# A gate's sigmoid rewritten as a tanh, its sum and its half moved into vector products

## The reference, cut to what matters

```python
# first block, end of the mLSTM branch: the output gate
hn = ((h - mu) * lax.rsqrt(var + EPS)) ... * norm_g
return jax.nn.sigmoid(o_pre) * hn                 # 512 channels

# second block, three branches mixed, each with its own gate of 1024 channels
y = sigmoid(g_a) * (short_conv @ w_sc_out)        # "ya"
  + sigmoid(g_b) * (stick_breaking @ w_sb_out)    # "yb"
  + sigmoid(g_c) * (ssm @ w_ssm_out)              # "yc"
h = y @ w_o
```

## Time and profile before

| | |
|---|---|
| time, median of 3 runs | 902.93 us (901.65 to 908.4) |
| the profiled execution | 907.06 us, span 905.3 us |
| PE busy | 860.5 us (95%) |
| DVE busy | 651.4 us (72%) |
| ACT busy | 503.7 us (56%), of it 43 table loads in the program |
| mean granted clock of PE | 0.97 of full |

### The profile page before, as it was taken

How to read it: one execution, slowest core, us unless ns; L and a number is a source line. 1 busy time by engine, 2 the same in 40 slices (tenths; PEclk the granted TensorE clock), 3 DMA queues, 4 the chain that set the end, 5 groups by cost and what they waited for, 6 DMA issues and landing times.

```text
span 905.3 us, 15843 instructions
## 1 busy us (share of the span) xinstructions
PE 860.5 (95%) x6396; PEld 810.8 (90%) x6396; DVE 651.4 (72%) x1011; ACT 503.7 (56%) x723; POOL 7.6 (1%) x17
## 2 busy tenths in 40 slices
PE   8899997999899999999997999999899899999997
PEld 7789986889799999999997899898899899999886
DVE  5765787678567988887867896787798766665553
ACT  5643447455447666655455756777657554444342
POOL 0200000000000000000000000000000000000000
PEclk9999999989998999999998999999999799999999
DMA  9974556756062665667862376455575177775751
GB/s 339 244 216 138 171 182 195 215 172 229 28 185 72 214 186 185 187 196 240 261 210 70 118 251 185 147 187 181 169 233 166 60 250 225 233 233 186 168 204 47
DMA packets 139592, 166.89 MB, mean 184 GB/s; under 512 B 5520, under 2 KB 123280, under 8 KB 139520
## 3 DMA queue, kind: packets, MB, share of 16 engines
q1 hardware_dynamic: 137712, 162.82, 57.0%
q0 software_dynamic: 720, 2.02, 1.2%
q10 hardware_dynamic: 1088, 1.05, 0.3%
HBM read 164.62 MB, written 1.25 MB: 183 GB/s over the span
## 4 chain that ended last, share of the span: by engine, by line
PE 32%; DVE 12%; ACT 8%; issue 3%; DVEq 0%; ACTq 0%
PE ps L512 32%; DVE lor L1595 5%; DVE FA L1595 3%; ACT hir L1096 2%; DVE FA L1598 1%; ACT L1434 1%; DVE INL L1595 0%; ACT X L1366 0%; DVE raw L1612 0%; ACT HIH L1372 0%; ACT FA L1434 0%; DVE FA L2256 0%; DVE FA L1601 0%; ACT FA L1476 0%; DVE X L1595 0%
## 5 line engine op out<-in xcount | busy, mean ns | idle before, releaser
L1595 DVE TENSOR_TENSOR lor<-raw,hir 128x1024 fp32r<-128x1024 f32 (+1 forms) x267 | 309.9, 1178 | 118.8 <-ACT hir L1096 112.6
L1096 ACT ACTIVATE hir<-raw 128x1024 fp32r<-128x1024 f32 (+1 forms) x257 | 260.2, 1032 | 125.1 <-PE ps L512 105.3
L512 PE MATMUL ps<-INH,hir 128*128 128x256 f32 (+1 forms) x1064 | 306.9, 288 | 4.2 <-ACT INH L1259 2.5
L512 PE MATMUL ps<-INH,lor 128*128 128x256 f32 (+1 forms) x1064 | 302.4, 284 | 2.8 <-DVE lor L1595 2.7
L512 PE MATMUL ps<-INL,hir 128*128 128x256 f32 (+1 forms) x1064 | 303.0, 285 | 1.4 <-DVE INL L1595 1.2
L512 PEld LDWEIGHTS ps<-INH,hir 128*128 128x128 f32 x1064 | 204.9, 193 | 7.4 <-issue 6.1
L512 PEld LDWEIGHTS ps<-INH,lor 128*128 128x128 f32 x1064 | 204.5, 192 | 4.9 <-DVE lor L1595 3.9
L512 PEld LDWEIGHTS ps<-INL,hir 128*128 128x128 f32 x1064 | 204.0, 192 | 2.4 <-DVE INL L1595 2.4
L512 PE MATMUL ps<-HIH,lor 128*128 128x256 f32 x688 | 195.5, 284 | 5.2 <-DVE lor L1595 5.2
L512 PE MATMUL ps<-HIH,hir 128*128 128x256 f32 x688 | 197.9, 288 | 0.0
L512 PE MATMUL ps<-HIL,hir 128*128 128x256 f32 x688 | 194.0, 282 | 0.0
(11 more groups left out here) (270 smaller groups left out, 793.6 us busy)
## 6 DMA issues: line engine op xcount, KB each, us to landing
raw<-in_w_in SPq DMA_DIRECT2D x64, 512.0 KB, 4.5
raw<-in_mod_wT SPq DMA_DIRECT2D x48, 512.0 KB, 4.5
raw<-in_ffn_w_up SPq DMA_DIRECT2D x44, 512.0 KB, 4.5
raw<-in_w_ffn_in SPq DMA_DIRECT2D x44, 512.0 KB, 4.8
raw<-in_w_ffn_out SPq DMA_DIRECT2D x22, 512.0 KB, 4.4
raw<-in_ffn_w_down SPq DMA_DIRECT2D x20, 512.0 KB, 5.0
raw<-in_xa_wkv SPq DMA_DIRECT2D x16, 512.0 KB, 3.8
raw<-in_xa_wq SPq DMA_DIRECT2D x8, 512.0 KB, 5.7
```

Source lines behind the costliest of these rows:

```text
L512: return e.matmul(o, l, r, start=start, stop=stop, skip_group_check=True)
L1096: e.activation(hi, src, ACT.Copy).then_inc(*w_hi.up(i))
L1595: return e.tensor_tensor(o, a, b, op)
```

## The change

Sigmoid(x) is written as (1 + tanh(x/2)) / 2. ACT stores t = tanh(x/2), by the scale 0.5 that an activation takes. DVE's product of gate and branch becomes (t + 1) · branch in one `stt`. The half is put in where the result is split: ACT's copy to `hi` takes scale 0.5, and DVE's `lo` is 0.5·value − `hi`, in one `stt` in place of a `tt`. For `OG`, the norm's weight, which was in the product with the gate, moves into the product ahead of it, with `rv`.

```diff
--- before.py
+++ after.py
@@ -1097,8 +1097,8 @@
 
             ahead = Ahead(plan, slot, split)
 
-            def put(x, k, n, src):
-                e.activation(x.hi[:, k:k + n, :], src, ACT.Copy).then_inc(*act.up(*x.his(k, n)))
+            def put(x, k, n, src, scale=1.0):
+                e.activation(x.hi[:, k:k + n, :], src, ACT.Copy, scale=scale).then_inc(*act.up(*x.his(k, n)))
 
             def conv(o, p, K, wname, bname, nb, i, key):
 
@@ -1150,7 +1150,7 @@
                 def o_gate(c):
                     yield from ahead.unit_g(("o", c), 8)
                     w.wait_ge(mm.at(("unit", ("o", c))))
-                    e.activation(OG[:, 2 * c:2 * c + 2, :], wide2(bank["unit", ("o", c)]), ACT.Sigmoid).then_inc(
+                    e.activation(OG[:, 2 * c:2 * c + 2, :], wide2(bank["unit", ("o", c)]), ACT.Tanh, scale=0.5).then_inc(
                         *act.up(("out", ("unit", ("o", c)))))
                     yield
 
@@ -1205,7 +1205,7 @@
                 e.activation(VR[hp], VR[hp], ACT.Sqrt).then_inc(*act.up(("deviation", hp)))
                 yield 1
                 w.wait_ge(dve.at(("OG", hp)))
-                put(mix, h0, 2, OG[:, h0:h0 + 2, :])
+                put(mix, h0, 2, OG[:, h0:h0 + 2, :], 0.5)
                 yield 1
 
             def swa(g):
@@ -1431,7 +1431,7 @@
                     yield from ahead.unit_g(("gl", c), 8)
                     dst = GLS[:, 2 * c:2 * c + 2, :] if c < 8 else GLC[:, 2 * c - 16:2 * c - 14, :]
                     w.wait_ge(mm.at(("unit", ("gl", c))), mm.at("before third norm"), dve.at("before third norm"), act.at("before third norm"))
-                    e.activation(dst, wide2(bank["unit", ("gl", c)]), ACT.Sigmoid).then_inc(*act.up(("out", ("unit", ("gl", c)))))
+                    e.activation(dst, wide2(bank["unit", ("gl", c)]), ACT.Tanh, scale=0.5).then_inc(*act.up(("out", ("unit", ("gl", c)))))
                     yield
 
                 def branch(key, c):
@@ -1503,7 +1503,7 @@
 
             def mg_put(c):
                 w.wait_ge(dve.at(("merged", c)))
-                put(mg, 2 * c, 2, GLC[:, 2 * c:2 * c + 2, :])
+                put(mg, 2 * c, 2, GLC[:, 2 * c:2 * c + 2, :], 0.5)
 
             for c in range(4):
                 ahead.unit(("yc", c), 4)
@@ -1632,9 +1632,12 @@
 
             ahead = Ahead(plan, slot, split)
 
-            def put(x, k, n, src):
+            def put(x, k, n, src, scale=None):
 
                 w.wait_ge(act.at((x.name, "hi", k + n - 1)))
+                if scale is not None:
+                    stt(x.lo[:, k:k + n, :], src, scale, x.hi[:, k:k + n, :].bitcast(F32), MUL, SUB).then_inc(*dve.up(*x.los(k, n)))
+                    return
                 tt(x.lo[:, k:k + n, :], src, x.hi[:, k:k + n, :].bitcast(F32), SUB).then_inc(*dve.up(*x.los(k, n)))
 
             def conv(o, p, K, wname, nb, i, key, *keys):
@@ -1757,11 +1760,13 @@
                 then("vc")
                 yield from across(("rv", hp), vc, DN)
                 w.wait_ge(mm.at(("rv", hp)))
-                tt(EM, EM, wide2(bank["rv", hp]), MUL).then_inc(*dve.up(("out", ("rv", hp))))
+                for h in range(2):
+                    stt(EM[:, h, :], EM[:, h, :], V("ml_norm_g", h0 + h), bank["rv", hp][:, h * T:(h + 1) * T], MUL, MUL).then_inc(
+                        *dve.up(("out", ("rv", hp))))
                 w.wait_ge(dve.last(), act.at(("out", ("unit", ("o", hp)))))
-                for h in range(2):
-                    stt(OG[:, h0 + h, :], EM[:, h, :], V("ml_norm_g", h0 + h), OG[:, h0 + h, :], MUL, MUL).then_inc(*dve.up(("OG", hp)))
-                put(mix, h0, 2, OG[:, h0:h0 + 2, :])
+                og = OG[:, h0:h0 + 2, :]
+                stt(og, og, 1.0, EM, ADD, MUL).then_inc(*dve.up(("OG", hp)))
+                put(mix, h0, 2, og, 0.5)
                 yield 1
 
             def swa(g):
@@ -2174,7 +2179,7 @@
                     yield from ahead.unit_g((key, c), 2)
                     dst = GLS[:, 2 * g:2 * g + 2, :]
                     w.wait_ge(mm.at(("unit", (key, c))), act.at(("out", ("unit", ("gl", g)))))
-                    tt(dst, dst, wide2(bank["unit", (key, c)]), MUL).then_inc(*dve.up(("branch", g), ("out", ("unit", (key, c)))))
+                    stt(dst, dst, 1.0, wide2(bank["unit", (key, c)]), ADD, MUL).then_inc(*dve.up(("branch", g), ("out", ("unit", (key, c)))))
                     yield
 
                 for c in range(4):
@@ -2279,13 +2284,13 @@
 
             def mg_put(c):
                 w.wait_ge(dve.at(("merged", c)))
-                put(mg, 2 * c, 2, GLC[:, 2 * c:2 * c + 2, :])
+                put(mg, 2 * c, 2, GLC[:, 2 * c:2 * c + 2, :], 0.5)
 
             for c in range(4):
                 ahead.unit(("yc", c), 4)
                 sgc = GLC[:, 2 * c:2 * c + 2, :]
                 w.wait_ge(mm.at(("unit", ("yc", c))), act.at(("out", ("unit", ("gl", 8 + c)))))
-                tt(sgc, sgc, wide2(bank["unit", ("yc", c)]), MUL).then_inc(*dve.up(("out", ("unit", ("yc", c)))))
+                stt(sgc, sgc, 1.0, wide2(bank["unit", ("yc", c)]), ADD, MUL).then_inc(*dve.up(("out", ("unit", ("yc", c)))))
                 w.wait_ge(dve.last(), dve.at(("branches", c)))
                 tt(sgc, GLS[:, 2 * c:2 * c + 2, :], sgc, ADD).then_inc(*dve.up(("merged", c)))
                 if c:
```

## The result

The changed kernel takes 901.69 us (median of 20 runs, 898.78 to 904.17), the kernel before 905.82 us (median of 20 runs, 901.65 to 908.49). The medians are 4.1 us apart; the ratio is 0.9951, with a 95% interval of 0.9939 to 0.9963: 4.4 us faster, between 3.4 and 5.5. The forecast was a gain of 4.9 us and a time of 898.0, counted from the three runs of the kernel before then shown. The measured time is in the stated range of 894 to 904, but 3.7 us above the forecast, mostly because the kernel before has a median of 905.82 over 20 runs and had one of 902.93 over those three.

A forecast was written before the change was run, and what follows sets the result against it. PE bounds the kernel. Output gates 0, stalls 1.03 + 0.39 + 0.56 + 0.9 to 1.4 and the clock's 1.8 us, taken as 4.9, off a median of 902.93 give 898.0 us; range 894 to 904.

The forecast's parts named there:

- D: PE's stall of 2.43 us in the second block's gates' stage, waiting for DVE's product; 1.0 to 1.5 us stays.
- The bound: PE, busy 860.5 of 905.3 us; in the second block's gates' stage it has 6.2 us to give.
- The output gate: First block's output gates, 60 to 105 us: PE never stands still there, so the load removed gains 0.
- DVE's work: Twelve products of gate and branch and six splits become `stt`: 0, with an upper bound of 1.2 us.
- A: PE's stall of 1.03 us in the second block's gates' stage, waiting for DVE's mask products; all of it goes.
- B: PE's stall of 0.39 us in the same stage, on a split that ACT and DVE deliver late; all goes.
- C: PE's stall of 0.56 us in the same stage, waiting for DVE's split of 631.78; all of it goes.
- The clock: Lower clock level behind D, about 638.6 to 642 us: its loss of 1.8 us goes, at about 7 in 10.
- the sum: Over the whole kernel, stall gains plus 0.7 of the 1.8 us clock loss: expected gain 4.1 to 4.7 us.
- likeliest case: Second block's gates' stage: the clock stays up behind D, gain 4.7 to 5.2 us, taken as 4.9.
- hidden loads: Rival, chance 0.20: loads mostly hidden, D keeps nearly all its length and clock loss; gain 1 to 2, time 901 to 902.

## Why the prediction was right

The mechanism held: loads go, PE's stalls in the gates' stage go with them, and what is left of D is DVE's own list. The sizes held less well, and two errors cancelled.

**The bound** was read rightly: the gain comes from what PE waits for in the gates' stage, and from nothing elsewhere. Of the 16.7 us of loads about a quarter reached the end.

**The output gate, and DVE's work, at nothing**: shown by the runs with each alone.

**Stalls A, B, C gone**: so it was. ACT's timeline of the change shows the steps of the working, as the earlier trace rows:

```profile
560.43 0.60 ACT L1434 ACTIVATE FA<-ps 128x512 f32<-128x512 f32 x1 [0.77 <-PE ps L512]
...
572.03 0.57 ACT L1434 ACTIVATE FA<-ps 128x512 f32<-128x512 f32 x1
574.60 0.85 ACT L1462 ACTIVATE FA<-FA 128x768 f32<-128x768 f32 x1 [1.99 <-DVE FA L1595]
...
607.18 1.04 ACT L1096 ACTIVATE hir<-raw 128x1024 fp32r<-128x1024 f32 x1
608.12 0.58 ACT L1434 ACTIVATE FA<-ps 128x512 f32<-128x512 f32 x1
608.72 1.28 ACT L1486 ACT_TABLE_LOAD   x1
...
625.97 0.58 ACT L1434 ACTIVATE FA<-ps 128x512 f32<-128x512 f32 x1
...
630.55 0.51 ACT L1475 ACTIVATE FA<-FA,small 128x256 f32<-128x256 f32 x1 [3.06 <-DVE FA L2245]
```

The gate at 572.03 is followed by the Exp without a load, and ACT now waits 1.99 us for DVE's sums, which end at 574.56:

```profile
573.55 1.01 DVE L1595 TENSOR_TENSOR FA<-FA,ps 128x512 f32<-128x512 f32 x2
...
625.14 0.96 DVE L1595 TENSOR_TENSOR FA<-FA 128x768 f32<-128x768 f32 x1 [1.56 <-ACT FA L1476]
626.02 1.22 DVE L1612 SCALAR_TENSOR_TENSOR raw<-raw,cb 128x1024 f32<-128x1024 f32 x1
...
627.16 2.35 DVE L1595 TENSOR_TENSOR lor<-raw,hir 128x1024 fp32r<-128x1024 f32 x2
629.43 0.75 DVE L1595 TENSOR_TENSOR FA<-ps,con 128x256 f32<-128x256 f32 x2
630.10 0.41 DVE L2245 COPY FA<-ps 128x256 f32<-128x256 f32 x1
632.07 0.96 DVE L1595 TENSOR_TENSOR FA<-FA 128x768 f32<-128x768 f32 x1 [1.56 <-ACT FA L1476]
```

As forecast, DVE's sums set the Exp at A. But they end only 0.55 us sooner in the stage (20.36 us from the first Abs before, 19.81 now), not 1.28: without its load the gate of `gl` 0 waits 0.77 us for PE's product (560.43 above), which I had left out. The Exp starts 1.29 us sooner (21.14 and 19.85) and not 1.9. It was still enough for A's 1.03 us.

What I mis-sized most is how much PE had to gain up to D: 1.98 us, by the idle times of the earlier trace rows, but it was 2.97 when it asked for D's product. The idle times are only those that the profile shows between two matmuls, and PE can be slow in windows that it shows as busy. Two windows of before just behind B, and the same part of PE's list in the change, whose matmul of 598.30 starts at 595.00:

```profile
598.00:600.00 2.00, 1.70 (x14) 1.70 (x15) 1.97 (x4) 1.97 (x4) 0.00 (x0) 1.00 0.25 62
600.00:602.00 2.00, 1.96 (x16) 1.75 (x16) 2.00 (x5) 1.99 (x3) 0.00 (x0) 1.00 0.99 299
```

```profile
595.00:599.00 4.00, 4.00 (x36) 4.00 (x35) 4.00 (x6) 3.99 (x5) 0.00 (x0) 1.00 0.78 225
```

The same 28 matmuls start between 598.30 and 602.01 before and between 595.00 and 598.32 in the change, at a clock of 1.00 in both. Since PE's list is the same, all its 6396 matmuls can be paired by their order like this. In the stage the change gains 1.10 us at A, 0.55 at B and 0.39 in the 4 us behind B, 0.14 on the way to C, 0.72 at C, 0.07 behind it and 0.76 at D: 3.73 in all, of which the recorded stalls explain 2.73 (1.03, 0.39, 0.56 and 2.43 − 1.68).

**Stall D**: forecast 1.0 to 1.5 us left, with a chain that gains 2.9 to 3.4; measured 1.68 left, with a chain that gained 3.72. The mechanism was that of the forecast: in the rows of DVE the two splits stand back to back from 627.16, with no idle time between, where DVE had waited 0.66 us. Both sizes were low. The first of the splits came 2.97 us sooner in the stage, where I had taken 2.2 to 2.7, and PE asked 2.97 us sooner in place of 1.98, the larger error; that the rest is DVE's list was only argued then, and is shown by moving its products.

**The clock**: taken at 1.8 us with 7 in 10. Its size was nearly right (1.6), but I took it as a loss in every execution of the kernel before, and of the four executions with such a stall only two had it. If that is its share, an estimate from four executions, it is worth 0.8 us and not the 1.3 of the sum or the 1.8 of the likeliest case. The 3.72 us behind D stay on PE: paired by order, and without the clock's loss behind D, its matmuls are 3.73 us ahead to the end of the stage. (The 3.4 us by the stage's length are less by 0.29 us of idle time of ACT, at 671.70, between two splits ahead of the Square that ends the stage.) So 3.7 + 0.8 make 4.5, against 4.4 measured, between 3.4 and 5.5.

**What was luck.** The stalls gave 3.7 us where 2.9 to 3.4 were forecast, and the clock 0.8 by that estimate where the forecast of 4.9 has 1.8. The two errors have opposite signs. The sum, weighted with my own 0.7, was 4.1 to 4.7, nearer to the measured 4.4 than the 4.9 that I took from its likeliest case.

Of the rivals, hidden loads came nearest: D kept 1.7 of 2.4 us, and 901.69 us lies in the 901 to 902 that it gave. But that is the kernel before being slower than its three runs; the gain is 4.4 us and not 1 to 2, A to C went with more than their recorded length, and the lower clock behind D did not stay.

## What to carry to other kernels

A table load stands where ACT's list passes from one table set to another. Here 13 of 43 could be taken out by writing a function as another one that the active set has anyway, because its constants fitted into scales and products that existed already. What that is worth is not loads times 1.28 us (16.7 us here, for a gain of 4.4): it is read from the stalls of the bounding engine, each traced back to whether a load or another engine's list stands last ahead of it. When a stall stays after the loads are gone, look at what else stands in the same list by mere habit of order, and move that to a stage with room.

## What the runs showed that I had not expected

Without a load ahead of it the gate's activation starts under the tail of the split before: at 608.12, 0.94 us after one of 1.04 us. It takes 588 ns in the mean where it was 599. The loads thus cost a little more than their 1283 ns, and ACT's busy time fell by 17.4 us and not by 16.7.

The same stall of 2.4 us had the lower clock behind it in two executions and full clock in two, and the clock withheld from the same program differed by about 9 us, the span by 6.0. For a change worth 4 us, the places in a stage, counted from a common instruction, tell more than the span: in the three profiles of the change PE has D's product at 78.34, 78.35 and 78.33 us.
